# A two-layer decoder trunk on one core: unit splits, scores and S5 recurrence of the second layer in another order

## The reference, cut to what matters

```python
for l in range(DEPTH):                                   # 2
    h = x @ w_in[l]                                      # 1024 -> 2956 columns
    s5_u, mq, mk, mv, gq, gk, gv, gz, ga, gb = _split(h, IN_SIZES)
    y_s5 = s5_mixer(s5_u, ...)
    y_moba = moba_mixer(mq, mk, mv)                      # softmax(q k^T) v, six heads
    y_gdn = gdn_mixer(gq, gk, gv, gz, ga, gb, conv_w[l], ...)
    mix = jnp.concatenate([y_s5, y_moba, y_gdn], -1) @ w_out[l]
    x = layer_norm(ALPHA * x + mix, ln1_g[l], ln1_b[l])
    f = swiglu(x, ...) if l % 2 == 0 else moe_ffn(x, ...)
    x = layer_norm(ALPHA * x + f, ln2_g[l], ln2_b[l])
```

## Time and profile before

| | |
|---|---|
| median of 3 runs | 1600.63 us (1598.14 to 1601.91) |
| profiled execution, on the device | 1601.82 us |
| its span from first to last instruction | 1599.9 us |
| dense mixer of layer 0 ends | about 424 us into the span |
| mixers of layer 1 | about 424 to 600 us |
| experts | from about 611 us to the end |

### The profile page before, as it was taken

How to read it: one execution, slowest core, us unless ns; L and a number is a source line. 1 busy time by engine, 2 the same in 40 slices (tenths; PEclk the granted TensorE clock), 3 DMA queues, 4 the chain that set the end, 5 groups by cost and what they waited for, 6 DMA issues and landing times.

```text
span 1599.9 us, 24154 instructions
## 1 busy us (share of the span) xinstructions
PE 1544.6 (97%) x9412; PEld 1274.1 (80%) x9412; DVE 1258.6 (79%) x1224; ACT 957.5 (60%) x811; POOL 100.0 (6%) x134
## 2 busy tenths in 40 slices
PE   8998999999897899999999999999999999999996
PEld 6777688888796776888888888888888888888875
DVE  6856754444867677888888888888888888888897
ACT  1175154443426443677777777777777777777774
POOL 0012180000000211000000000000000000000200
PEclk9999999999998999999999999999999999999998
DMA  9412488785242224999999999999999999999994
GB/s 331 160 54 81 176 317 294 277 288 186 79 153 87 108 81 153 383 395 392 398 393 363 398 393 351 397 393 353 396 394 352 395 395 351 395 395 370 397 394 163
DMA packets 195770, 473.12 MB, mean 296 GB/s; under 512 B 7713, under 2 KB 22177, under 8 KB 194641
## 3 DMA queue, kind: packets, MB, share of 16 engines
q1 hardware_dynamic: 191552, 454.23, 76.5%
q0 software_dynamic: 4144, 17.88, 2.9%
HBM read 464.21 MB, written 25.69 MB: 306 GB/s over the span
## 4 chain that ended last, share of the span: by engine, by line
PE 88%; DVE 7%; ACT 2%; issue 2%; DMA 1%; SPq 0%; DVEq 0%; ACTq 0%; POOLq 0%
PE ps L1847 47%; PE ps L1858 23%; PE ps L1797 4%; PE ps L1920 2%; DVE unit_lo L1294 1%; PE ps L1825 1%; PE ps L2313 1%; PE ps L2309 1%; PE ps L1809 1%; DVE arena L1196 1%; DMA arena<-in_w_in 1%; PE ps L1817 1%; PE ps L2209 1%; PE ps L2200 0%; PE ps L2119 0%
## 5 line engine op out<-in xcount | busy, mean ns | idle before, releaser
L1288 DVE TENSOR_TENSOR lo<-arena,hi 128x2048 fp32r<-128x2048 f32 x378 | 865.3, 2292 | 205.5 <-ACT hi L732 205.1
L732 ACT ACTIVATE hi<-arena 128x2048 fp32r<-128x2048 f32 x378 | 724.4, 1919 | 353.8 <-PE ps L1847 228.4
L1847 PE MATMUL ps<-hi,xg 128*128 128x512 f32 x1760 | 542.7, 390 | 0.0
L1847 PEld LDWEIGHTS ps<-hi,xg 128*128 128x128 f32 x1760 | 329.6, 188 | 68.2 <-DVE lo L1288 0.2
L1847 PE MATMUL ps<-lo,xg 128*128 128x512 f32 x880 | 342.4, 389 | 0.0
L1858 PE MATMUL ps<-hi,hTe 128*128 128x512 f32 x896 | 282.4, 396 | 0.0
L1847 PEld LDWEIGHTS ps<-lo,xg 128*128 128x128 f32 x880 | 165.2, 188 | 34.3
L1858 PEld LDWEIGHTS ps<-hi,hTe 128*128 128x128 f32 x896 | 164.1, 188 | 32.0
L1858 PE MATMUL ps<-lo,hTe 128*128 128x512 f32 x448 | 175.1, 391 | 0.0
L1847 PE MATMUL ps<-hi,xs 128*128 128x512 f32 x512 | 159.7, 393 | 2.1 <-DVE xs L1603 1.1
L1847 PEld LDWEIGHTS ps<-hi,xs 128*128 128x128 f32 x512 | 96.2, 189 | 22.2 <-issue 2.5
(11 more groups left out here) (417 smaller groups left out, 1573.8 us busy)
## 6 DMA issues: line engine op xcount, KB each, us to landing
arena<-in_mg SPq DMA_DIRECT2D x112, 1024.0 KB, 7.8
arena<-in_mu SPq DMA_DIRECT2D x112, 1024.0 KB, 8.3
arena<-in_md SPq DMA_DIRECT2D x112, 1024.0 KB, 7.9
arena<-in_wg SPq DMA_DIRECT2D x14, 1024.0 KB, 6.0
arena<-in_wu SPq DMA_DIRECT2D x14, 1024.0 KB, 5.8
arena<-in_wd SPq DMA_DIRECT2D x14, 1024.0 KB, 5.0
arena<-in_w_in SPq DMA_DIRECT2D x10, 1024.0 KB, 5.5
xg_rows<-in_zeros SPq DMA_DIRECT2D x17, 512.0 KB, 6.8
```

The costliest lines, as they stand in the source:

```text
L732: af(hi[r % PARTS][:, :], raw[r % RAWS], ACT.Copy).then_inc(hi_ready, 1)
L1288: tt(lo[r % PARTS][:, :], raw[r % RAWS], hi[r % PARTS][:, :].bitcast(F32), ALU.subtract)\
L1847: ins = mm(ps[:, (4 if w == "G" else 4 + nb) + b, :], tok[a][:, kk * nt + b * P:kk * nt + (b + 1) * P], tiles_of(part[r % PARTS], w)[:, k, ...
```

## The change

Nothing is added to or taken from the computation; the same instructions run in another order.

- Ahead of `norm(1, ...)` VectorE makes the low part of unit 0 alone (before: units 0 to 3). Unit 1's follows `rows_low`, those of units 2, 3 and 4 follow `s5_matrices`.
- VectorE takes the scores between the turn of the first S5 half and the recurrence of the second, with the low parts of units 6 and 7 ahead of them and 8 and 9 behind. The convolution follows in one piece after the second turn, then the low part of unit 10.
- TensorE computes the scores behind unit 5 (before: behind unit 6).
- Units 8 and 9 change places in the table, and so in the order of loading, of high parts and of low parts: the 396 columns of z, a, b are now unit 8, the last 256-column gate unit is 9. TensorE still multiplies the gate unit first.
- ScalarE's `unit_high(4)` now stands before the evacuation of the S5 input, 5 and 6 behind that of unit 2, 7 behind that of unit 3, 8 between evacuations 6 and 7, 10 behind the division of the scores.

```diff
@@ UNITS
+         (C_Z, ZAB, A_RAW, A_RAW + KT * ZAB),
          (C_G + 768, 256, A_PHASE + PIECE, A_RAW + 4 * PIECE),
-         (C_Z, ZAB, A_RAW, A_RAW + KT * ZAB),
@@ ScalarE
+                if l:
+                    unit_high(4)
                 evac(2 * l, (uT, ...))
                 if l:
                     stepped_matrices()
-                    unit_high(4)
                 evac(2 * l + 1, (qkm[:, 0:2, :], ps[:, 5, :]))
                 if l:
                     unit_high(5)
+                    unit_high(6)
                 evac(2 * l + 2, (qkm[:, 2:4, :], ps[:, 2, :]))
...
-                    unit_high(6)
+                    unit_high(7)
...
-                else:
-                    unit_high(7)
                 evac(6, (cin[:, 0:2, 3:259], ...))
+                if l:
+                    unit_high(8)
                 evac(7, (cin[:, 2:4, 3:259], ...))
                 if l:
-                    unit_high(8)
                     unit_high(9)
...
                 evac(8, (cin[:, 4:6, 3:259], ...))
-                if l:
-                    unit_high(10)
...
                 ins.then_inc(sc_norm, 1)
+                if l:
+                    unit_high(10)
@@ VectorE
                     for q in range(4):
                         rows_low(q)
+                    unit_low(1)
...
+                    unit_low(2)
+                    unit_low(3)
                     unit_low(4)
-                s5_rotate(l, 0)
...
+                    s5_rotate(l, 0)
+                    s5_rotate(l, 1)
                     unit_low(5)
+                    s5_recur(l, 0)
+                    s5_turn(l, 0)
                     unit_low(6)
                     unit_low(7)
+                    scores()
                     unit_low(8)
                     unit_low(9)
+                    s5_recur(l, 1)
+                    s5_turn(l, 1)
+                    score_sums_turned()
+                    convolve(l, 0)
+                    convolve(l, 2)
+                    convolve(l, 4)
                     unit_low(10)
...
                     channel_mixer()
-                    for n in range(READY):
-                        unit_low(n)
+                    unit_low(0)
                     norm(1, (0, 1, 2, 3), ...)
@@ TensorE
                     split_features(6, 5).then_inc(proj_psum, 1)
+                    scores()
                     split_features(7, 6).then_inc(proj_psum, 1)
...
-                    split_features(7, 8).then_inc(proj_psum, 1)
+                    split_features(7, 9).then_inc(proj_psum, 1)
                     pe.wait_ge(sc_evac, 2 * NH)
-                    pe.wait_ge(unit_lo_ready, 10)
-                    split_tokens(5, 9, 0, SPLIT, True, True).then_inc(proj_psum, 1)
-                    split_tokens(4, 9, 1, SPLIT, True, True).then_inc(proj_psum, 1)
+                    pe.wait_ge(unit_lo_ready, 9)
+                    split_tokens(5, 8, 0, SPLIT, True, True).then_inc(proj_psum, 1)
+                    split_tokens(4, 8, 1, SPLIT, True, True).then_inc(proj_psum, 1)
```

More of the change, by code:

```diff
@@ L1380, in _, with scores @@
                 step(v_.memset(cin[:, :, 0:3], 0.0))
-                if l:
+                def scores():
+                    for h in range(NH):
+                        bank = (2, 3, 0, 1, 4, 5)[h]
+                        dve.wait_ge(sc_psum, NH * l + h + 1)
+                        step(stt(sc[:, h, 0:P], ps[:, bank, 0:P], SCALE, C("causal"), ALU.mult, ALU.add))
+                        step(ts(sc[:, h, P:2 * P], ps[:, bank, P:2 * P], SCALE, None, ALU.mult))
+                        stt(sc[:, h, 2 * P:3 * P], ps[:, bank, 2 * P:3 * P], SCALE, C("causal"), ALU.mult, ALU.add)\
+                            .then_inc(sc_evac, 1)
+                    dve.wait_ge(sc_evac, NH * (l + 1))
+                    step.wait()
+                    step(v_.tensor_reduce(nmax[:, 0:6], sc[:, :, 0:P], AX_X, ALU.max))
+                    step.then(v_.tensor_reduce(nmax[:, 6:12], sc[:, :, P:3 * P], AX_X, ALU.max))
+                    ts(nmax, nmax, -1.0, None, ALU.mult).then_inc(sc_max, 1)
@@ new lines, in score_sums_turned @@
+                def score_sums_turned():
+                    dve.wait_ge(sc_exp, 2 * NH * (l + 1))
+                    v_.reciprocal(rinv, rsum).then_inc(sc_norm, 1)
+                if l == 0:
+                    s5_rotate(l, 0)
[9 more added lines that the diff above has]
+                    convolve(l, 4)
+                else:
+                    unit_low(2)
+                    unit_low(3)
@@ L1382, in _ @@
                     unit_low(4)
-                s5_rotate(l, 0)
-                s5_rotate(l, 1)
-                if l:
+                    s5_rotate(l, 0)
+                    s5_rotate(l, 1)
                     unit_low(5)
-                s5_recur(l, 0)
-                s5_turn(l, 0)
-                if l:
+                    s5_recur(l, 0)
+                    s5_turn(l, 0)
                     unit_low(6)
-                s5_recur(l, 1)
-                s5_turn(l, 1)
-                if l:
@@ L1394, in _ @@
                     unit_low(7)
-                convolve(l, 0)
-                if l:
+                    scores()
                     unit_low(8)
                     unit_low(9)
[L1400 to L1415, removed]
+                    s5_recur(l, 1)
@@ L1416, in _ @@
+                    s5_turn(l, 1)
+                    score_sums_turned()
+                    convolve(l, 0)
+                    convolve(l, 2)
+                    convolve(l, 4)
                     unit_low(10)
-                convolve(l, 4)
                 gates_in(l)
@@ L1993, in s5_in, with scores @@
                     ins.then_inc(bu_psum, 1)
+                def scores():
+                    pe.wait_ge(proj_evac, 13 * l + 6)
+                    pe.wait_ge(bu_used, 2 * l + 2)
+                    for h in range(NH):
+                        bank = (2, 3, 0, 1, 4, 5)[h]
+                        j, rows = h // 2, slice(64 * (h % 2), 64 * (h % 2) + 64)
+                        mm(ps[:, bank, 0:P], qkm[rows, j, 0:P], qkm[rows, 3 + j, 0:P], start=True, stop=True)
+                        mm(ps[:, bank, P:3 * P], qkm[rows, j, P:T], qkm[rows, 3 + j, :], start=True, stop=True)\
+                            .then_inc(sc_psum, 1)
                 if l == 0:
```

## The result

The changed kernel took 1584.96 us, the median of 7 runs (1582.53 to 1590.84); the kernel before, in 7 runs of the same comparison, 1598.57. The ratio is 0.9914 with a 95% interval of 0.9894 to 0.9933: 13.6 us faster, with 10.7 to 16.9 us inside the interval. The forecast was 1588.5 us and 12.1 us; the measured time lies 0.5 us under the range.

What follows compares the result with a forecast made beforehand. TensorE is busy 97%, so only its 4.15 and 9.89 us holes, both released late by VectorE, could pay. Norm products gain 6.2 + 1.87 + 1.13 + 1.23 + 0.87 + 0.8 = 12.1 us: median 1588.5, range 1585.5 to 1593 (own range 1587 to 1590).

Steps and rivals of the forecast that it cites:

- The opening at full clock: After the dense mixer, TensorE transposes block 0 without a wait at full clock; unit 0's sixteen products end at 428.9.
- the moved low parts at no cost: Low parts moved behind the norm fit where VectorE stood idle for 9.68 + 3.13 us, so they cost nothing.
- the scores without a wait: VectorE asks for the first head at 471.9; TensorE runs the scores from 469.9 to 472.2, so no wait.
- the row sums in time: Exponentials end at 487.1, VectorE asks for row sums at 489.1; its 1.87 us wait goes.
- Rival 2: Opening after the dense mixer stays at half clock: transposes and sixteen products keep their old times, -9.3 us; chance 0.12.
- Rival 3: Mixer order does not pay: VectorE waits for scores, high part 9 or exponentials, gain only -6 to -7 us; chance 0.10.
- Rival 4: Unit 4's load lands late, delaying S5 input and rotations one for one; kernel slower, 1604.6 us; chance 0.03.
- How the numbers follow: Step from gain to time: -12.1 us gives 1589.7 for the profiled execution, 1588.5 for the median; chance 0.54.
- a microsecond either way: Allowance for later half-clock stretches that may fall elsewhere in the execution.
- Rival 1: Clock holds over the shorter hole ahead of the norm products, which run at full clock: -14.1 us, 1586.5; chance 0.20.

Runs made afterwards that it cites:

- before, kept at full clock: Kernel before, with idle TensorE products: four ahead of the transposes, eleven ahead of the norm products; 1592.72 us against 1597.85, ratio 0.9964.
- lighter VectorE chain: Whole change, with first taps of channels 0 to 5 and unmasked scores moved to ScalarE and the Square halved; 1578.05 us, ratio to kernel before 0.9868.
- whole change, third: The change as it stands, run a third time against the kernel before; 1588.21 us against 1597.68, ratio 0.9936.
- whole change, again: The change as it stands, run a second time against the kernel before; 1590.19 us against 1598.20, ratio 0.9942.
- part 1 alone: Kernel before, with only unit 0's low part ahead of the last norm and 1 to 3 behind it; 1593.16 us against 1598.20, ratio 0.9960.

## Why the prediction was right or wrong

**The places were right.** From the dense mixer's end, forecast and measured: rotations 28.55 and 28.64; VectorE asks for the first head 47.85 and 47.89; norm products 79.05 and 79.22, forecast to move by 12.1 and moved by 11.95. VectorE's stretch 48.1 and 48.05, its busy time 46.96 and 46.92; TensorE's wait for the Square 4.5 and 4.55, for unit 9's low part 0 to 0.5 and 0.16. The opening at full clock, the moved low parts at no cost, the scores without a wait and the row sums in time are all in the rows after. Rivals 2, 3 and 4 did not come about.

Two readings in the rivals were off. Before, the sixteen products of unit 0 did not run at half clock throughout: PEclk is 0.50 from 433 to 434 us and 0.99 from 434 to 435, and they end at 435.41. And the norm products were priced at 2.4 us less at full clock; with idle products they took 2.05 less.

**What failed is the step from the places to the time**, in "How the numbers follow". 1600.63 less 12.1 is 3.6 us above the measured 1584.96. Of this 2.1 us are the level: the kernel before took 1598.57 in the same comparison and not 1600.63. The other 1.5 us are the gain, 13.6 instead of 12.1, and these cannot be told from chance: the interval of the gain is 10.7 to 16.9 us, and over 20 runs it is 11.0. Two terms were mis-sized.

1. *The level.* I took 1600.63 us, the median of the three runs shown, as if it were sharp. The 52 runs of that kernel reach from 1591.64 to 1605.02, with a median of 1597.9. From there 12.1 us lead to 1585.8, already at the lower end of the stated range.
2. *The time outside the changed stage.* I allowed "a microsecond either way", and only for stretches at half clock. Between the thirteen traces the dense mixer's end varies from 419.43 to 424.05 us, and the way from the norm products to the first product of the experts from 89.96 to 97.84 us. From there to the end they agree within 1.5 us (987.3 to 988.7).

The two profiled executions show what these variations are made of. Ahead of the change the one of before is 4.62 us late. Of this 3.04 us had come up by the following product of layer 0 (before, then after):

```profile
126.56 0.53 PE L2200 MATMUL ps<-arena 64*64 64x64 f32 x16 [2.44 <-DVE arena L1501]
...
123.52 0.46 PE L2224 MATMUL ps<-arena 64*64 64x64 f32 x16 [2.44 <-DVE arena L1520]
```

The loads make 1.67 us of it: before, TensorE waits 2.15 us for its load of x until 8.77 and starts the first projection at 11.87, after at 10.20 without that wait. The rest is the speed of its first matmuls. Before, there are 12 of them in the 5 us from 12 on and 20 in the 4 us from 18; after, 7 in the 2.8 us from 10.2 and already 20 in the 4 us from 14 (the PEclk column shows 1.00 all the while). The remaining 1.6 us are a stretch at half clock: from 126 to 131 us PEclk is 0.66 before. Behind the norm products it is clock almost throughout, since the time grows with TensorE's busy time for the same matmuls and not with its idle time:

| trace | norm products to experts, us | TensorE busy | idle | PEclk |
|---|---|---|---|---|
| before, kept at full clock | 89.96 | 81.52 | 8.44 | 1.00 |
| lighter VectorE chain | 91.18 | 81.56 | 9.62 | 1.00 |
| after | 94.07 | 84.47 | 9.60 | 0.97 |
| whole change, third | 95.69 | 86.13 | 9.56 | 0.95 |
| before | 96.48 | 86.63 | 9.85 | 0.94 |
| whole change, again | 96.96 | 87.22 | 9.74 | 0.93 |

The work is the same in all. The three traces of the whole change spread over 2.9 us here, with standstills equal to 0.2 us.

The pooled median of the change, 1587.39 us, lies within the stated range; the first comparison's 1584.96 does not. That the first seven runs fell 2.9 us under the mean of the next thirteen was luck.

**Rival 1 was framed too narrowly.** I asked only whether the norm products behind the shorter hole run at full clock. They do not: they take 4.20, 5.46 and 4.40 us in the three traces of the whole change, 4.86 before and 2.81 at full clock. What I left out is the clock of the whole execution, which rose with the change from 0.9885 to 0.9917 on average. Kept at full clock, the two kernels are 9.2 us apart; without, 11.0. The difference suggests that about 2 of the 11 us are clock and not order, but with standard errors of 1.0 and 0.8 it is not shown. Within my 12.1, 1.1 us of the opening were clock as well (91.17 against 90.06), and this the traces show.

**What stays open.** Why one execution keeps full clock through the delta rule and the next does not: its standstills there add up to nearly the same in all kernels (last table). And what share of the mean gain is clock: besides the 9.2 and 11.0 us, runs at 0.990 differ by 7.2 us between the two kernels, but that mean also counts half clock during standstills.

## What to carry to other kernels

When three engines meet at one wait, follow each one's queue back from it, and move work only out of the one that arrives last. Its unbroken chain then gives the new time (here within 0.2 us), provided that the second-latest is sized too (here 0.87 us behind), since it is the limit as soon as the first is shortened. And check that each thing that the moved step needs is moved with it, as the scores were here.

Standstill of TensorE is paid twice where the clock falls in it. Filling two holes with products that nobody reads gave 5.1 us, near half of what the reordering gave; before a hole is filled with real work, this is a cheap way to learn what it costs.

Take the level and the scatter from many runs, sorted by granted clock, before giving a range; one profile of before and three times do not carry 0.2%. Line up two traces at an event ahead of the change and at one behind it: here they differed by 4.6 us before the changed stage began, through a later load and a lower clock.

## What the runs showed of the hardware that was not expected

- The time of one kernel on one core varied by 13.4 us (1591.64 to 1605.02 in 52 runs) with the mean granted clock between 0.984 and 0.991, 1.2 us for each 0.001. Runs of equal clock (0.991) still differed by 5.0 us.
- In the changed stage TensorE's clock fell in all twelve standstills of 4.15 us or more in the traces without idle products (from 4.15 in the kernel before to 9.92 with part 1 alone), and it did not in those of 0.94, 1.52 and 3.02 us ahead of the norm products. But length alone does not tell: behind the halt of 2.44 us in layer 0, the same in all thirteen traces, the clock fell in five and not in eight. Behind a halt of 1.95 us in the changed kernel with idle products it fell too.
- Idle products kept the clock up in a hole: 1.00 in the 9.60 us where it was 0.69 on average before.
- Idle products cost nothing measurable where they end before the wait does: with 0.25 and 0.44 us of wait left, the norm products stayed at 79.25 and came 1.11 us earlier.
